# A hybrid decoder step on one core: two gate chunks loaded into the eleventh expert place, and four gate products ahead of the samples' scores

## What is computed

```python
xn = rmsnorm(x); proj = xn @ w_in                       # 1024 x 5888, columns split among the parts below
o_a = HGRN2(silu(hq), 1 - f, hi, log f, state_hgrn)      # 4 heads, chunkwise
o_b = RWKV7(r, decay, k, v, kk, a, state_rwkv)           # 8 heads of 64
merged = sigmoid(gate_a) * (o_a @ w_branch_a) + sigmoid(gate_b) * (o_b @ w_branch_b)
x = x + merged @ w_out
x = x + moe_top4_of_32(rmsnorm(x))                       # every expert: w_gu 1024 x 2048, w_down 1024 x 1024
y = rmsnorm(x)
```

## Time and profile before

| what | us |
|---|---|
| median of 3 runs | 1316.26 (1314.9 to 1321.04) |
| the profiled execution | 1315.85 |
| its span | 1314.0 |
| TensorE busy | 1284.8 (98%) |
| VectorE, ScalarE, GpSimd busy | 372.8, 241.6, 56.6 |
| moved by DMA | 449.40 MB, mean 342 GB/s |

### The profile page before, as it was taken

How to read it: one execution, slowest core, us unless ns; L and a number is a source line. 1 busy time by engine, 2 the same in 40 slices (tenths; PEclk the granted TensorE clock), 3 DMA queues, 4 the chain that set the end, 5 groups by cost and what they waited for, 6 DMA issues and landing times.

```text
span 1314.0 us, 18370 instructions
## 1 busy us (share of the span) xinstructions
PE 1284.8 (98%) x7357; PEld 613.8 (47%) x7357; DVE 372.8 (28%) x1016; ACT 241.6 (18%) x532; POOL 56.6 (4%) x131
## 2 busy tenths in 40 slices
PE   9999999999999999999999999999999999999997
PEld 6778778888744333333333333333333333233333
DVE  3234756554327121121221211212112111211112
ACT  3144343222122110111111110111101101110102
POOL 5000200000060000000000000000000000000000
PEclk9999999999999999999999999999999999999999
DMA  7635437111879999999999999999999999999996
GB/s 237 172 98 192 134 81 274 36 34 34 307 279 379 428 429 428 428 428 428 430 428 428 427 430 431 430 429 429 429 429 431 430 430 430 429 429 430 430 429 265
DMA packets 73252, 449.40 MB, mean 342 GB/s; under 512 B 14408, under 2 KB 43130, under 8 KB 47884
## 3 DMA queue, kind: packets, MB, share of 16 engines
q1 hardware_dynamic: 67462, 445.45, 82.8%
q10 hardware_dynamic: 5734, 3.14, 0.8%
HBM read 443.82 MB, written 4.76 MB: 341 GB/s over the span
## 4 chain that ended last, share of the span: by engine, by line
PE 81%; DMA 14%; DVE 2%; ACT 2%; issue 0%; ACTq 0%; SPq 0%; DVEq 0%
PE bank L1288 26%; PE bank L1309 13%; DMA arena<-in_expert_w_gu_dram 7%; DMA ring<-in_expert_w_gu_dram 7%; PE bank L568 7%; PE bank L1203 5%; PE bank L658 5%; PE bank L1234 5%; PE bank L1082 2%; PE bank L1056 2%; PE bank L949 2%; ACT arena L1433 1%; PE bank L1210 1%; PE bank L1278 1%; PE bank L932 1%; PE bank L615 1%
## 5 line engine op out<-in xcount | busy, mean ns | idle before, releaser
L1288 PE MATMUL bank<-ring,arena 128*64 128x512 f32 x1040 | 233.6, 594 | 4.9 <-DMA ring<-in_expert_w_gu_dram 4.9
L1433 ACT ACTIVATE arena<-bank 128x512 f32<-128x512 f32 (+7 forms) x233 | 115.1, 514 | 479.2 <-PE bank L1309 196.2
L1288 PE MATMUL bank<-arena 128*64 128x512 f32 x768 | 173.3, 594 | 2.4 <-DMA arena<-in_expert_w_gu_dram 2.4
L1433 ACT ACTIVATE arena<-arena 128x256 f32<-128x256 f32 (+7 forms) x124 | 68.9, 564 | 468.9 <-DVE arena L2394 461.4
L1288 PEld LDWEIGHTS bank<-ring,arena 128*64 128x64 f32 x1040 | 72.8, 137 | 146.2 <-issue 122.8
L2394 DVE TENSOR_SCALAR arena<-bank 128x256 f32<-128x256 f32 x64 | 26.9, 421 | 375.5 <-PE bank L1288 375.5
L1309 PE MATMUL bank<-ring,arena 128*64 128x512 f32 x544 | 121.9, 595 | 0.0
L2440 DVE COPY arena<-bank 64x512 f32<-64x512 f32 x30 | 20.8, 693 | 318.5 <-PE bank L1309 318.5
L1288 PEld LDWEIGHTS bank<-arena 128*64 128x64 f32 x768 | 53.9, 137 | 105.8 <-issue 92.6
L1203 PE MATMUL bank<-arena 128*64 128x512 f32 x372 | 89.6, 599 | 0.0
L568 PE MATMUL bank<-arena,ring 128*128 128x296 f32 (+1 forms) x352 | 87.6, 411 | 0.0
(11 more groups left out here) (374 smaller groups left out, 1127.0 us busy)
## 6 DMA issues: line engine op xcount, KB each, us to landing
ring<-in_expert_w_gu_dram SPq DMA_DIRECT2D x63, 2048.0 KB, 23.6
arena<-in_expert_w_gu_dram SPq DMA_DIRECT2D x47, 2048.0 KB, 23.0
ring<-in_expert_w_down_dram SPq DMA_DIRECT2D x35, 2048.0 KB, 23.6
arena<-in_expert_w_down_dram SPq DMA_DIRECT2D x21, 2048.0 KB, 24.6
extra<-in_expert_w_gu_dram SPq DMA_DIRECT2D x15, 2048.0 KB, 25.7
ring<-in_w_in_dram SPq DMA_DIRECT2D x23, 1024.0 KB, 5.2
extra<-in_expert_w_down_dram SPq DMA_DIRECT2D x6, 2048.0 KB, 25.6
ring<-in_w_out_dram SPq DMA_DIRECT2D x4, 1024.0 KB, 7.4
```

The lines of the kernel that those rows point to most:

```text
L1288: ins = mm(bank[q % 2][64 * (q // 2):64 * (q // 2) + 64, :], gu_lhs(c), w[:, q * 512:(q + 1) * 512], start=(c == 0), stop=(c == KT - 1), s ...
L1433: return nc.scalar.activation(out, in_, f, **kw)
```

## The change

Gate chunks 15 and 16 (`AHEAD`) are loaded into the two halves of `extra` where `w_load(sp, 1, 10)` stood. They signal on `wo_loaded`, the semaphores of chunks 29 and 30, which then count to 32. The expert chunk of place 10 is loaded once the groups of chunk 16 are done, ahead of the outputs of the RWKV states. Chunks 17 to 20 take the ring slots after chunks 13, 14, 11 and 12. The wait for the samples' scores ahead of chunk 16 goes. `smp_scores` begins with `gate(4)`; the `gate(3)` ahead of the first half of L704 goes, and the one between the halves becomes `gate(2)`.

```diff
+        AHEAD = (15, 16)
+
+        def mix_signal(n):
+
+            if n < N_IN + 6 and n not in AHEAD:
+                return ring_loaded[n % RING_MIX], 16 * sum(m not in AHEAD for m in range(n % RING_MIX, n + 1, RING_MIX))
+            x = n - AHEAD[0] if n in AHEAD else n - N_IN - 6
+            return wo_loaded[x], 16 if n in AHEAD else 32
+
         def mix_chunk(n):
 
             s = (n + 3) % RING_MIX if n < N_IN + 6 else n - (N_IN + 6) + RING_MIX
-            slot = ring[:, s * CH:(s + 1) * CH]
+            slot = ring[:, s * CH:(s + 1) * CH] if n not in AHEAD else extra[:, (n - AHEAD[0]) * CH:(n - AHEAD[0] + 1) * CH]
...
-            for n in list(range(EARLY)) + [N_IN + 6, N_IN + 7] + list(range(EARLY, N_IN + 6)):
+            for n in [n for n in range(EARLY) if n not in AHEAD] + [N_IN + 6, N_IN + 7] + list(range(EARLY, N_IN + 6)):
...
-                if n >= RING_MIX and n < N_IN + 6:
+                if n >= RING_MIX and n < N_IN + 6 and n != 21:
                     m = n - RING_MIX
+                    if m in AHEAD:
+                        m -= RING_MIX
...
-                if n == 16:
-                    sp.wait_ge(S("smp_pe"), smp_pe["scores"] + 2)
-                if n == 20:
+                if n == 21:
+                    sp.wait_ge(S("pj_done"), pj_after(AHEAD[1]))
+                    w_load(sp, 1, 10)
                     sp.wait_ge(S("smp_act"), smp_act["out"] + 4)
                     for b in range(NB):
                         src, dst = smp_state(S0T, rwkv_s, b)
                         sp.dma_start(dst, src).then_inc(S("rws_out"), 16)
+                    sp.wait_ge(S("pj_done"), pj_after(n - RING_MIX))
                 dst, src = mix_chunk(n)
-                sp.dma_start(dst, src).then_inc(ring_loaded[n % RING_MIX] if n < N_IN + 6 else wo_loaded[n - N_IN - 6], 16)
+                sp.dma_start(dst, src).then_inc(mix_signal(n)[0], 16)
...
-                    w_load(sp, 1, 10)
+                    for a in AHEAD:
+                        dst, src = mix_chunk(a)
+                        sp.dma_start(dst, src).then_inc(mix_signal(a)[0], 16)
...
             def chunk_ready(n):
-                if n < N_IN + 6:
-                    pe.wait_ge(ring_loaded[n % RING_MIX], 16 * (n // RING_MIX + 1))
-                else:
-                    pe.wait_ge(wo_loaded[n - N_IN - 6], 16)
+                pe.wait_ge(*mix_signal(n))
...
             def smp_scores():
 
+                gate(4)
                 pe.wait_ge(S("smp_dve"), smp_dve["ins"] + 1)
...
-                gate(3)
                 for G in range(2):
                     if G:
-                        gate(3)
+                        gate(2)
```

## The result

The changed kernel takes **1320.13 us** (median of 22 runs, 1317.07 to 1324.6) against 1316.10 (22 runs, 1314.9 to 1321.28) of the kernel before: ratio 1.0035, 95% interval 1.0025 to 1.0045. It is 4.0 us slower where 0.6 us less was forecast. That is still under the 0.5% named in the prediction, but outside its range, 1313.3 to 1319.0, and on the other side of zero.

A forecast was written before the change was run, and what follows sets the result against it. The prediction took TensorE to bound the mixer and the DMA queue the tail. Its terms, -0.63 + 0 + 0 + 0, taken from the 1316.26 us median, gave 1315.6 us, range 1313.3 to 1319.0.

The forecast's parts named there:

- The wait: At the samples' scores: gate products begin at 144.48, where scores began at 145.11; 0.47 of the 1.1 us wait remain.
- The size of the gain: TensorE begins 0.63 us earlier at the samples' scores, the only nonzero term of the sum.
- The upper bound of the term, 1.1: At the samples' scores: the saving if all of the 1.1 us wait goes.
- The rival of more gain: Whole 1.1 us wait at the scores and 0.6 us of later VectorE waits go: 1.7 us, 1314.6; chance 0.07.
- The changes between kinds of products stay as many, so I cost them at nothing: Mixer: one gate block less behind the scores, one more ahead, so reordering TensorE's products costs 0.
- everything from there on is 0.63 us early: From the solve on, the four moved products are paid back; first solve product at 155.11 for 155.74.
- Chunks 15 to 20, "price 0": Mixer gate chunks: 15 and 16 land around 125, 17 to 20 by 156 or so, before their readers; price 0.
- What the later scores hold up: Behind the scores, which begin 1.57 us later: VectorE's masks, ScalarE's copies and GpSimd's work stay covered; price 0.
- The expert chunk and the late state output: 187 to 208 us: 2 MB load delays the second HGRN output 2.9 us, to 211.0; TensorE doesn't wait, price 0.
- The 11 us rival: State outputs: the 2 MB cost 11 us, not 5.9; output at 219, 5.2 us net loss; late-output case chance 0.07.
- From the mixer to the end: What TensorE saves in the mixer, 0.63 us, also shifts the DMA queue's full-rate stretch and so the kernel's end.
- Within 0.5%: Whole kernel: no change beyond 0.5% (6.6 us) either way, chance 0.93; faster 0.03, slower 0.04.

The follow-up runs named there:

- e7: The changed kernel with 1, 2, 3, 2 gate products ahead of scores, first half, second half, solve; chunk 18 held until scores done: 1315.18 us, ratio 0.9997.
- e4: The changed kernel with three gate products between the halves and one ahead of the solve, in place of two and two: 1322.64 us, ratio 1.0056.
- e10: The kernel before with one gate product moved from between the halves to ahead of the first half: 1320.30 us, ratio 1.0025.
- e9: The changed kernel with three gate products between the halves in place of two, and four in place of five in the solve: 1315.84 us, ratio 1.0008.
- e1: The change's loads with the gate products where the kernel before had them: 1315.73 us, ratio 1.0004.
- e3: The changed kernel with chunk 18 held until the samples' scores are done, cutting the burst of loads in two: 1317.55 us, ratio 1.0008.
- e8: The changed kernel with eight throwaway 128x128 products ahead of the first half of the products with the copied states: 1320.55 us, ratio 1.0033.
- e5: The changed kernel with the two gate products ahead of the solve moved ahead of the first half: 1319.37 us, ratio 1.0017.

## Why the prediction was wrong

**The wait.** Right: 0.63 us saved at the first product ahead of the scores, 0.47 us left (0.47 measured), first scores forecast at 146.7 and found at 146.59.

**The size of the gain.** Mis-sized, the other way: 1.07 for 0.63. From the first score to the work behind the stacked operands the kernel before took 2.33 us (145.11 to 147.44), the changed one 1.89 (146.59 to 148.48). The second four scores wait for the second copy to `S0T` and the stacked operands for the third; I counted only the wait for the first. In the kernel before, the four copies take turns of about 0.5 us, and each of these pieces starts as its copy ends (ACT's copies, second scores, first operands):

```profile
144.37 2.06 ACT L1433 ACTIVATE ring<-bank 128x512 f32<-128x512 f32 x4
145.50 0.34 PE L686 MATMUL bank<-arena 64*32 64x64 f32 x8
145.99 0.30 PE L694 MATMUL bank<-arena 64*32 64x64 f32 x2
```

From the first score to the first operand that makes 0.88 us, and 0.48 in the changed kernel (146.59 to 147.07), where the copies are done. With one product ahead, in e7, the whole piece still takes 2.30 us (144.91 to 147.21). The upper bound of the term, 1.1, had the size, but as the wait of 1.1 us gone, of which 0.47 stayed; so that it fits is luck. The rival of more gain said 1.7 us, with 0.6 from the two later waits, which are as they were (0.4 and 0.2).

**"The changes between kinds of products stay as many, so I cost them at nothing", and "everything from there on is 0.63 us early".** This is the step that failed: the overlap costed at 0 came to 4.17 us, 0.92 in the break and 3.25 at half clock, and the kernel was 3.08 us late at RWKV in place of 0.63 early. The step takes a product's duration as fixed, whatever stands around it. I checked for each moved product who waits for it, and never what the piece that it left looks like without it. The gate products weren't only work in need of a place. With three of them between the halves the clock held in all profiles but e4's, with two it fell (e10: one product moved, its median 4.2 us above that of the kernel before). They also set when the second half begins, and with the burst an early start brings the break (e4, e9: 0.42 us with a third product in front of it, for 0.92). No rival named either.

**Chunks 15 to 20, "price 0".** Wrong in one respect. No product waited for them, which e1 confirms. But the wait for the samples' scores that the change takes away had also cut the burst of loads in two, and with the new order the uncut burst brought the break of 0.92 us (e3, without it, has none).

The Trainium skill (Runtime: NRT & Kernel Launch, Instruction fetch mechanics) says that an engine's sequencer fetches its next block of 256 instructions (16 KiB) by a DMA of its own while it executes the current one, and that the cost is mostly hidden. The packets above, some 16 KB each, agree with the size; how many instructions one holds no run here shows. If the reading of the break is right, the 0.92 us at L715 is a place where the cost wasn't hidden.

**What the later scores hold up.** Right in its verdict. One reading in it is wrong: the first half of L704 comes behind one gate product more than before (four for three), not fewer. By the prediction's own terms it would still not be later (0.63 saved, 0.55 added), and it began at 148.48 for 149.09.

**The expert chunk and the late state output.** Right in its verdict: TensorE waited for neither. The 11 us rival did not come, though the outputs took twice as long to issue. The second HGRN output was there at 208.5 (201.11 and 7.4), where 211.0 was forecast, in a mixer 3 us late.

**From the mixer to the end.** Right, with the sign turned: 3.08 us late at RWKV, 3.09 at the first load behind the logits (394.94 for 391.85), 3.18 at the last product. The waits of the tail for expert chunks are as before (5.0 us for 4.9 in the largest group), so here the end took over all that the mixer lost.

**Range and chances.** The forecast time and the range missed. "Within 0.5%" at 0.93 held, since the loss is 0.35%, but by the small size of the loss and not by the reasons given for it.

## What to carry to other kernels

Large products between tiny ones need not be free filler: before one is moved, look at the piece it leaves and at the granted clock there, and try the move alone in the old kernel. A wait in a load queue that seems to guard nothing may keep a burst of loads apart that costs TensorE a break, as here. And where runs come in groups, read the mean clock of each run before comparing medians.

## What the runs showed of the hardware

- TensorE's clock fell to half for 6.8 us in a stretch in which TensorE was busy all the time by the profile but for a break of 0.92 us, and in e10 (10.2 us) and e3 (6.8 us) without any break.
- Sixteen passes of 128x128 right ahead of the tiny products (e8) did not keep the clock up; one gate product more between them (e9) did in seven runs of ten.
- One packet of the instruction queue came some 2 us later under a burst of 4 MB, and TensorE stood for 0.92 us (0.42 in e4 and e9) in a stream of passes that start every 0.03 us; that the one caused the other is inferred.
- The kernel before itself is some 4 us slower, with a lower mean clock, in 26 of its 147 runs, which the profile of a good run doesn't show. That this is a fall near 400 us is inferred from the profiles of e1, e4, e5 and e10.
- Eight outputs of 128 KB took 14.14 us to issue on SP behind a load of 2 MB, for 6.65 without it; in e1, with the same loads, 14.14 as well.
